# Block 0's back projection: two column blocks as seven half-size products, their weight sums made in the kernel

## The reference, cut to what matters

```python
y = jnp.concatenate([y_att, y_conv, y_pool], axis=-1)   # (1, 512, 2048)
y = jnp.einsum('bse,ed->bsd', y, w_out[l])              # back projection
x = layer_norm(DEEPNORM_ALPHA * x + y, ln_g[l], ln_b[l])
```

## Time and profile before

| | |
|---|---|
| timed runs, median of 3 | 1711.92 us (1711.91 to 1712.26) |
| span of the profiled execution | 1710.5 us, 21921 instructions |
| its own time | not given beside the span |
| DVE, ACT, POOL busy | 760.0, 632.7, 700.2 us |
| mean granted TensorE clock | 0.998 of full |
| DMA | 186.16 MB, mean 109 GB/s |

### The profile page before, as it was taken

How to read it: one execution, slowest core, us unless ns; L and a number is a source line. 1 busy time by engine, 2 the same in 40 slices (tenths; PEclk the granted TensorE clock), 3 DMA queues, 4 the chain that set the end, 5 groups by cost and what they waited for, 6 DMA issues and landing times.

```text
span 1710.5 us, 21921 instructions
## 1 busy us (share of the span) xinstructions
PE 1697.0 (99%) x7998; PEld 1394.2 (82%) x7998; DVE 760.0 (44%) x1268; ACT 632.7 (37%) x884; POOL 700.2 (41%) x300
## 2 busy tenths in 40 slices
PE   9999999999999999999999999999999999999997
PEld 6888888888888888888888888888668888888886
DVE  6323321222111134211662745648789854566226
ACT  6434433444222224212552333334452544462120
POOL 4433343333444444445244434334236333326451
PEclk9999999999999999999999999999999999999999
DMA  6323223322333332533253442434223222227332
GB/s 237 112 91 93 93 86 93 96 90 89 102 97 92 95 97 86 172 123 99 65 208 111 135 128 95 130 104 124 62 75 98 87 74 74 86 62 271 123 98 99
DMA packets 56223, 186.16 MB, mean 109 GB/s; under 512 B 5928, under 2 KB 6184, under 8 KB 55376
## 3 DMA queue, kind: packets, MB, share of 16 engines
q1 hardware_dynamic: 46512, 160.19, 30.4%
q10 hardware_dynamic: 9632, 24.88, 4.2%
HBM read 176.57 MB, written 8.47 MB: 108 GB/s over the span
## 4 chain that ended last, share of the span: by engine, by line
PE 98%; DVE 1%; ACT 0%; DMA 0%; issue 0%; SPq 0%; DVEq 0%; ACTq 0%
PE bank L472 96%; PE bank L476 2%; DVE feats L1350 0%; DMA feats<-in_x_t 0%; DVE planes_lo L1562 0%; DVE bank L1555 0%; ACT w_hi L899 0%; ACT bank L1139 0%; DVE stats L1513 0%; ACT feats L1121 0%; DVE planes_lo L1361 0%; ACT planes_hi L945 0%; ACT planes_hi L1145 0%; DVE mv L1542 0%; SPq L346 0%
## 5 line engine op out<-in xcount | busy, mean ns | idle before, releaser
L425 POOL TENSOR_TENSOR w_lo<-raw,w_hi 128x1024 fp32r<-128x1024 f32 x272 | 667.3, 2455 | 969.6 <-ACT w_hi L899 969.6
L472 PE MATMUL bank<-planes_hi,w_hi 128*128 128x512 f32 (+1 forms) x1776 | 694.6, 391 | 1.7 <-ACT planes_hi L945 1.2
L472 PE MATMUL bank<-planes_hi,w_lo 128*128 128x512 f32 (+1 forms) x1776 | 685.3, 386 | 0.0
L472 PE MATMUL bank<-planes_lo,w_hi 128*128 128x512 f32 (+1 forms) x1776 | 684.7, 386 | 0.1
L899 ACT ACTIVATE w_hi<-raw 128x1024 fp32r<-128x1024 f32 x276 | 292.8, 1061 | 906.7 <-PE bank L472 866.7
L472 PEld LDWEIGHTS bank<-planes_hi,w_hi 128*128 128x128 f32 x1776 | 333.6, 188 | 84.5 <-issue 17.2
L472 PEld LDWEIGHTS bank<-planes_hi,w_lo 128*128 128x128 f32 x1776 | 333.6, 188 | 68.1
L472 PEld LDWEIGHTS bank<-planes_lo,w_hi 128*128 128x128 f32 x1776 | 333.8, 188 | 67.1 <-DVE planes_lo L1361 1.3
L472 PE MATMUL bank<-w_hi,planes_hi 128*128 128x512 f32 x480 | 187.6, 391 | 0.0
L472 PE MATMUL bank<-w_hi,planes_lo 128*128 128x512 f32 x480 | 186.8, 389 | 0.0
L472 PE MATMUL bank<-w_lo,planes_hi 128*128 128x512 f32 x480 | 186.8, 389 | 0.0
(11 more groups left out here) (293 smaller groups left out, 1404.8 us busy)
## 6 DMA issues: line engine op xcount, KB each, us to landing
raw<-in_stream SPq DMA_DIRECT2D x281, 512.0 KB, 3.6
h_rows<-feats ACTq DMA_DIRECT2D x4, 1024.0 KB, 9.1
feats<-in_x_t SPq DMA_DIRECT2D x7, 512.0 KB, 8.9
out<-feats ACTq DMA_DIRECT2D x7, 512.0 KB, 2.7
rope_q<-cum_dram ACTq DMA_DIRECT2D x8, 256.0 KB, 3.2
bias<-in_x_rows ACTq DMA_DIRECT2D x2, 1024.0 KB, 6.3
probs<-in_x_rows ACTq DMA_DIRECT2D x2, 1024.0 KB, 8.0
rope_q<-decay_dram SPq DMA_DIRECT2D x8, 256.0 KB, 5.6
```

Of the source, the lines that this page charges most:

```text
L425: nc.gpsimd.tensor_sub(w_lo[:, s, :], raw[:, s, :], w_hi[:, s, :].bitcast(fp32)).then_inc(lo_ready, 1)
L472: return nc.tensor.matmul(o, a, b, start=start, stop=stop)
```

## The change

Planes and weights of the first two column blocks are split in quarters: tokens 0 to 255 and 256 to 511 (left and right half of each plane), planes 0 to 7 and 8 to 15, column blocks 0 and 1. The product of two 2x2 matrices of quarters is made of seven products in place of eight (Strassen's form, with Winograd's sums). Each is 256 tokens x 1024 channels x 512 columns: four units, and per unit 2 planes x 2 token blocks x 3 = 12 matmuls. Three of the seven take quarters of the planes (A11, A12, A22), four take sums of quarters (S1 to S4). The order is A11, A12, S2, S3, S1, A22, S4. Some products are added on in PSUM to what stands in a bank.

- **Weight sums.** Four of the seven need sums of weight quarters. SP loads the four units that belong together into `bias` and `probs` (`load_pair`), DVE makes four sums after each of the four convolutions (`sum_pair`, 128x1024 each), SP stores them in DRAM (`store_sums`, 4 x 4 units, 8.4 MB in and as much out). Units 8 to 23 of the back projection are read from there; the stream has 12 units fewer for block 0's back projection, four of them at its end, and the offsets of later loads move.
- **Plane sums.** DVE makes S1, S3, S2, S4 in place in `feats` (`sum_planes`, 16 operations of 128x2x256), three of them before it takes the last pooling product, ACT rounds them (`cut_sum`), DVE makes their low parts (`low_sum`, 8 operations of 128x4x256).
- **Order.** EARLY for block 0 is 8, not 4. Six more cuts stand on DVE before the last feature. The pooling matmul stands after unit 1. ACT rounds each unit under its own number (`round_back`), unit 2 before the early cuts, unit 3 after the last take. The takes are `part` (residual plus a partial product, kept in the residual) and `whole`.
- The third and fourth column blocks are made as before, with other tile numbers (BLOCK2, BLOCK3); block 1 is as before.

```diff
+BLOCK2 = [14, 8]
+BLOCK3 = [BLOCK2[0] + 4, BLOCK2[1] + 4]
+BACK_LAST = [BLOCK3[0] + 4, BLOCK3[1] + 4]
+SEVEN = ["A11", "A12", "S2", "S3", "S1", "A22", "S4"]
+SUMS_FROM, SUMS_TO = 8, 24
...
-BACK_ORDER = [list(range(12)) + [15, 14, 13, 12], list(range(4)) + list(range(8, 16)) + list(range(4, 8))]
-EARLY = 4
+BACK_ORDER = [list(range(12)) + [14, 15, 12, 13], list(range(4)) + list(range(8, 16)) + list(range(4, 8))]
+EARLY = [8, 4]
...
+            def load_pair(u):
+
+                sp.wait_ge(feat_done, HEADS) if u == 0 else sp.wait_ge(sums_stored, 64 * u)
+                for src, dst in zip((first_pair, stream.shape[0] - 4, first_pair + 4, first_pair + 8), pair_units):
+                    sp.dma_start(dst, stream[src + u:src + u + 1, :, :].rearrange("u p n -> p (u n)")).then_inc(pair_loaded, 16)
...
+            def store_sums(u):
+
+                sp.wait_ge(sums_made, u + 1)
+                for k, src in zip((0, 2, 3, 1), pair_units):
+                    sp.dma_start(sums_dram[4 * k + u:4 * k + u + 1, :, :].rearrange("u p n -> p (u n)"), src).then_inc(sums_stored, 16)
...
+            def load_back(tile, u):
+
+                m, s = tile // 2, 2 * (tile % 2) + u
+                n = 2 * (tile - T_BACK1) + u
+                if not SUMS_FROM <= n < SUMS_TO:
+                    load_next(m, s, MADE if n >= SUMS_TO else 0)
+                    return
+                if n == SUMS_FROM:
+                    sp.wait_ge(sums_stored, 64 * 4)
+                sp.wait_ge(lo_ready, 4 * m + s - 7)
+                sp.dma_start(raw[:, s, :], sums_dram[n - SUMS_FROM:n - SUMS_FROM + 1, :, :].rearrange("u p n -> p (u n)"))\
+                    .then_inc(raw_loaded[s], 16)
...
+            for tile in range(pair_tile, T_MISC):
+                u, after = divmod(tile - pair_tile, 4)
+                if u < 4 and after == 0:
+                    load_pair(u)
+                if u < 4 and after == 2:
+                    store_sums(u)
+                load_back(tile, 0)
+                load_back(tile, 1)
...
+            def project_seven(first, after_unit):
+
+                for n, of in enumerate(SEVEN):
+                    if of == "S2":
+                        pe.wait_ge(feat_done, 16)
+                    if of == "S3":
+                        pe.wait_ge(parts_taken, 4)
+                    if of == "S1":
+                        pe.wait_ge(parts_taken, 6)
+                    if of == "A22":
+                        pe.wait_ge(parts_taken, 8)
+                    if of == "S4":
+                        pe.wait_ge(rows_taken, 4)
+                    dst = {"A11": FROM_LEFT, "S3": FROM_LEFT, "A22": FROM_LEFT, "A12": LOWER}.get(of, FROM_ALL)
+                    fresh = of in ("A11", "A12", "S2")
+                    for u in range(4):
+                        m, p = tile_at(first, 2 * n + u // 2)
+                        s = 2 * p + u % 2
+                        pe.wait_ge(lo_ready, 4 * m + s - 3)
+                        if of[0] == "S" and u % 2 == 0:
+                            pe.wait_ge(sums_ready, 2 * ("S2", "S3", "S1", "S4").index(of) + u // 2 + 1)
+                        for k in range(2):
+                            e = BACK_ORDER[0][2 * u + k + (UK if of in ("A12", "A22", "S1", "S4") else 0)]
+                            if of in ("A11", "A12"):
+                                pe.wait_ge(planes_ready, 16 + 2 * u + k + (UK if of == "A12" else 0) + 1)
+                            hi, lo = w_hi[:, s, S * k:S * k + S], w_lo[:, s, S * k:S * k + S]
+                            for i in range(2):
+                                if of[0] == "A":
+                                    rows = slice(P * i + (2 * P if of == "A22" else 0), P * i + (2 * P if of == "A22" else 0) + P)
+                                    a_hi, a_lo = planes_hi[:, e, rows], planes_lo[:, e, rows]
+                                else:
+                                    rows, b = slice(P * i, P * i + P), 0 if of in ("S2", "S1") else 1
+                                    a_hi, a_lo = sum_hi[b][:, e % UK, rows], sum_lo[b][:, e % UK, rows]
+                                end = u == 3 and k == 1
+                                mm(dst[i][:, :], a_hi, hi, fresh and u == 0 and k == 0, False, not fresh)
+                                mm(dst[i][:, :], a_hi, lo, False, False, not fresh)
+                                last = mm(dst[i][:, :], a_lo, hi, False, end, not fresh)
+                        last.then_inc(unit_used, 1)
...
+                    else:
+                        act.wait_ge(unit_used, 2 * (T_BACK1 + BLOCK2[0]))
...
                 else:
+                    round_unit(t[0] + 1, 2 * t[1])
                     cut_early(0, T_BACK1)
...
+                def round_back(n):
+                    m, p = tile_at(first, n // 2)
+                    round_unit(m, 2 * p + n % 2)
+
+                def cut_sum(n, dst, src):
+
+                    act.wait_ge(planes_summed, ("S1", "S3", "S2", "S4").index(n) + 1)
+                    for h in range(2):
+                        signal(nc.scalar.activation(dst[:, 4 * h:4 * h + 4, :], src[:, 4 * h:4 * h + 4, :], ACT.Copy), sum_cut,
+                               2 * ("S2", "S3", "S1", "S4").index(n) + h + 1)
...
-                        after_cut[n]()
+                if blk == 0:
+                    round_back(3)
+                    act.wait_ge(feat_done, 15)
+                    for n in range(UK, KT):
+                        if n == 12:
+                            round_back(4)
+                        if n == 14:
+                            round_back(5)
+                            act.wait_ge(feat_done, 16)
+                        cut_hi(BACK_ORDER[0][n], 16 + n + 1)
...
                 if blk:
                     act.wait_ge(rows_stored, STORED[0])
+                else:
+                    round_back(6)
+                    act.wait_ge(sums_stored, 64 * 4)
                 load_resid(0)
                 load_resid(1)
+                if blk == 0:
+                    for n in range(7, 2 * BLOCK2[0]):
+                        round_back(n)
+                        if n == 8:
+                            cut_sum("S2", sum_hi[0], feats[:, 0:UK, 0:S // 2])
+                        if n == 9:
+                            cut_sum("S3", sum_hi[1], feats[:, 0:UK, S // 2:S])
+                        if n == 15:
+                            cut_sum("S1", sum_hi[0], feats[:, UK:KT, S // 2:S])
+                        if n == 19:
+                            cut_sum("S4", sum_hi[1], feats[:, UK:KT, 0:S // 2])
+                    act.wait_ge(rows_taken, 6)
+                    load_resid(2)
...
-                for db in range(4):
+                for db in range(0 if blk else 2, 4):
                     if db in (1, 2):
                         act.wait_ge(rows_taken, 16 * blk + 4 * db)
                         load_resid(db + 1)
                     if db == 3:
                         round_end(blk)
+                    elif blk == 0:
+                        for n in range(2 * BLOCK2[0], 2 * BLOCK3[0] + 4):
+                            round_back(n)
...
+
+                dve.wait_ge(pair_loaded, 64 * (u + 1))
+                b11, b12, b21, b22 = pair_units
+                step(V.tensor_sub(b22, b22, b12))
+                step(V.tensor_sub(b12, b12, b11))
+                step(V.tensor_add(b11, b11, b22))
+                signal(V.tensor_sub(b21, b21, b11), sums_made, u + 1)
...
+            with step.loop(0, 4, 8) as j:
                 conv_mixer(j)
...
+                sum_pair(j)
...
+            def sum_planes(n, u):
+
+                a, b = BACK_ORDER[0][2 * u], BACK_ORDER[0][UK + 2 * u]
+                left, right = slice(0, S // 2), slice(S // 2, S)
+                a11, a21 = feats[:, a:a + 2, left], feats[:, a:a + 2, right]
+                a12, a22 = feats[:, b:b + 2, left], feats[:, b:b + 2, right]
+                if n == "S1":
+                    ins = V.tensor_add(a22, a21, a22)
+                elif n == "S3":
+                    ins = V.tensor_sub(a21, a11, a21)
+                elif n == "S2":
+                    ins = V.tensor_sub(a11, a22, a11)
+                else:
+                    ins = V.tensor_sub(a12, a12, a11)
+                if u < 3:
+                    step(ins)
+                else:
+                    signal(ins, planes_summed, ("S1", "S3", "S2", "S4").index(n) + 1)
...
                 signal(V.tensor_sub(tmp[:, 0:w - 1], tmp[:, 0:w - 1], padded[:, 16:16 + w - 1]), pool_in, n + 1)
+                if g == 0:
+                    cut_back(0, EARLY[0], KT - 2)
+                    for u in range(3):
+                        sum_planes("S1", u)
...
-            cut_back(0, EARLY, KT)
+            cut_back(0, KT - 2, KT)
...
+                def low_sum(n):
+
+                    v, b, src = {"S2": (0, 0, feats[:, 0:UK, 0:S // 2]), "S3": (1, 1, feats[:, 0:UK, S // 2:S]),
```

(82 more changed lines are left out.)

79 lines of the change are left out of this document (43 added, 36 removed).

## The result

The changed kernel takes 1729.13 us (median of 4 runs, 1728.86 to 1730.08) against 1712.07 for the one before in the same job: ratio 1.0100, 95% interval 1.0088 to 1.0112, 17.1 us slower. The forecast was 1730.4.

The account below looks back on a forecast made before the run. TensorE, 99% busy, was taken as the bound. The stage's 87.9 - 10.9 + 16.6 + 4.2 = 97.8, + 6.6 + 2.0 = 106.4, is +18.5 on 1711.9: 1730.4 us; range 1712 to 1740 (own 1721 to 1738).

Parts of the forecast that it names:

- Delay 1: Pooling matmul after unit 1: DVE's pooling chain collides with POOL's units 4 and 5, so TensorE stands 7.0 us.
- Delay 2: S2's first low part, at unit 8: DVE's plane work collides with POOL, TensorE 16.6 us late, Delay 1 included.
- Delay 3: Units 8 to 27: low parts of sums go between POOL's units; 4.2 us more, bounds 2 to 6.
- Delay 4: Turn to third block: ACT waits for the last take after S4 before rounding unit 28; TensorE stands 6.6 us.
- clock after it: After the stand before the third block, 4.1 us at half pace: 2.0 us lost, bounds 0 to 4.1.
- At nothing: Weight sums in DVE's idle time after each convolution, SP's stands at stores, and unit loads by DMA: no cost.

Follow-up runs that it names:

- e3: Changed kernel with POOL making only 64 of 1024 columns of the low parts of units 2 to 27 (rest left out): 1714.63 us.
- e1: Changed kernel with units 28 to 31 rounded before ACT's wait for the last take after S4: 1720.19 us.
- e2: Changed kernel with 26 matmuls of unused result filling TensorE's stand before the third column block: 1727.00 us.
- e4: Changed kernel with the pooling chain moved ahead, after four plane cuts instead of eight: 1729.08 us.
- e7: Changed kernel with the edits of e6, e4, e5 and e1 together: 1723.28 us.
- e11: e9 with unit 18's low part given back to POOL, leaving 12 on VectorE: 1712.79 us, ratio 1.0005 to the kernel before.
- e10: Changed kernel in a written-out order, each operation where TensorE needs it, all low parts of weights on POOL: 1722.45 us.
- e9: e10's order with 13 of the 26 low parts of weights made by VectorE instead of POOL: 1712.20 us, ratio 1.0000 to the kernel before.
- e5: Changed kernel with S4's four high sums moved behind the four moves out of A11 and A12: 1731.66 us.
- e6: Changed kernel with A22 taken third, before S2, in banks of its own: 1726.88 us.

## Why the prediction was right

On the axis of the trace, predicted and measured:

| step | predicted | measured |
|---|---|---|
| matmuls | 48 fewer, -10.9 | 48 fewer |
| Delay 1, pooling matmul | stands 7.0, to 679.3 | 6.5, to 679.01 |
| Delay 2, first of S2 | 706.1, 16.6 late | 705.63, 16.1 late |
| Delay 3, from there to the stage's end | 54.4 + 4.2 | 57.5, so +3.1 |
| Delay 4, third block | 6.6 | 6.5 |
| clock after it | 2.0 | 1.9 |
| sum | +18.5 | +16.7 (spans 1710.5 and 1727.2) |

**Delays 1 and 2** came out by the mechanism given: VectorE waits for the end of POOL's operation, whatever its own size. e3 shows it by taking POOL's time away. The Trainium skill ("SBUF — State Buffer", section "SBUF: two separate sides") calls this an exclusive lock for the instruction's duration. The 2.18 us for one number per partition, ended 0.02 after POOL's unit 5 (678.77 and 678.75), agree with it. The measurement parts from it in one thing: a pair of operations that alternate takes 2.77 us and not 0.69 + 2.39 = 3.08, so some 0.3 us of a VectorE operation did not wait.

**Delay 3** was mis-sized by 1.1 us, and its parts were others. Of the 3.1 measured, 0.6 is the slow pace of S3 and S4, which I did not know of, and some 1.5 the slow clock after the second stand (705.6 to 708.8), which I had said would be lost inside waits. Of the remaining 1.0, two short hitches make 0.8: 0.45 at S3's first two matmuls (718.44), where TensorE waited for VectorE's last take of A11 as the prediction said it would, and 0.36 at A22's first two (740.93). POOL's units against low parts, of which I made all 4.2, show at most in the second. So the step "POOL against the low parts" did not happen as described, and the size was in its bounds of 2 to 6 by luck.

**Delay 4 and the clock**: shown by e1 and e2 separately. The stand is only the order of ScalarE's list, and 8.9 of the 17.1 us are bought back by four roundings moved up.

**At nothing** held. The first convolution's four sums end at 464.2, before the 472 I allowed (one collision, 3.30 for 1.23). SP stands 2.0 us at each of the four stores until the sums are there, which TensorE does not feel: the back projection starts at 666.9 as before.

```profile
459.61 3.30 DVE L1623 TENSOR_TENSOR bias<-bias,probs 128x1024 f32<-128x1024 f32 x1
462.94 1.22 DVE L1624 TENSOR_TENSOR probs<-probs,bias 128x1024 f32<-128x1024 f32 x1
```

**What the prediction did not see** is that the path was full as a whole. I reckoned delays one by one, as if each were a misplaced operation. Between 662.85 and 738.50 POOL makes 19 low parts (19 x 2.39 = 45.4) and VectorE has 33.7 us of two-input work at its free durations: 16 cuts and 16 sums at 0.69, 8 low parts at 1.23, the chain's 1.7. That is 79.1 us in a stretch of 75.65, possible only since a pair that alternates takes 2.77 and not 3.08. The two engines' timelines agree: in all but 1.9 us of that stretch one of them is at such an operation, where before 30.6 us were free. It fits e4, e7 and e11, where a stand removed comes back elsewhere, and the 10.25 us between e10 and e9. That no order could have done better than e1 is not shown; none of the five tried did (e4 to e7 and e10). The same stretch of before, then of after, by windows (POOL's time and count stand before the clock):

```profile
662.85:738.50 75.65, 75.65 (x333) 62.28 (x332) 26.46 (x29) 24.46 (x30) 33.92 (x14) 1.00 0.42 134
```

```profile
662.85:738.50 75.65, 62.59 (x252) 49.62 (x251) 70.83 (x57) 39.64 (x45) 51.71 (x19) 0.89 0.44 146
```

19 low parts for 14 are 12.0 us more, 24 more operations of VectorE are 16 x 0.69 + 8 x 1.23 = 20.9 more, so the path owed about 46 of 75.65 before. By this account that is where the 10.9 us went: the 48 matmuls were bought with 33 us on a path that had 29 to spare, and the stage was to be shorter by 10.9 as well. The third stand has nothing to do with the path; it is the order of ScalarE's list.

## What to carry to other kernels

Before you give work to an engine that looks half idle, add up what its operations and those of the engine that it shares a path with owe in the stretch in question, at their free durations, and compare with what TensorE needs for it. If the sum is near the stretch, expect little of another order: here an edit that mended one stand mostly moved it (nothing in e4, 2.5 lost in e5, 2.2 won in e6). What gave most was an operation made by the engine that does it in less time of the path (10.25), and filling an idle stretch of the path instead of leaving it (2.87 us for four sums, not 10.71). Fewer matmuls are a gain only as long as the operands for each come as cheaply.

## What the runs showed of the hardware

- The same high and low matmul starts every 0.2267 or every 0.2333 us, by where in SBUF its stationary operand lies; a shift of 64 bytes changed nothing, an exchange of tiles moved it.
- The clock fell from 2.4 to 1.2 GHz 2.1, 2.7 and 3.5 us after the work ended at the three stands (and 4.1 at the kernel's end), and came back 5.9, 3.1 and 4.0 us after the restart (679.01 to 684.9, 705.63 to 708.8, 769.63 to 773.6). Two shorter stands cost clock too, with the fall just after the restart: 2.2 us (e3, before S2: low from 692.2 to 695.6) and 2.9 us (e5, low from 731.7 to 735.1). One of 2.3 us (e10, to 688.37) cost none.
- POOL and VectorE with both queues full: a 512-element operation of VectorE takes 2.77 to 2.81 us beside 0.69 free, a 1024-element one 3.30 beside 1.23, one with one number per partition 2.18 beside 0.16. A collision adds 2.0 to 2.1 us whatever VectorE's size, close to POOL's 2.39.
